# A layer's norm weight moved into its weight blocks, and rows turned by a product with a diagonal matrix

## The reference

```
for l in range(2):
    h = x * rsqrt(mean(x*x, -1) + 1e-6) * pre_norm_g[l]
    l == 0:  proj = h @ w_in_ab;  y = concat(diff_attention * silu(ga), sliding_window * silu(gb)) @ w_out_ab
    l == 1:  proj = h @ w_in_c    (q, k, v, gate: 4 x 1024 columns)
             y = (chunked attention of 16 heads, band of 9 chunks, relative bias) * silu(gate) @ w_out_c
    x = x + (y * rsqrt(mean(y*y, -1) + 1e-6) * post_norm_g[l])
```

## Time and profile before

| what | value |
|---|---|
| median of 3 runs | 1218.73 us (1218.23 to 1219.78) |
| the profiled execution's own time | 1218.22 us |
| its span | 1216.4 us |
| granted PE clock, mean | 0.995 of full speed |
| PE, DVE, ACT, POOL busy | 1186.4, 805.5, 589.1, 432.4 us |
| L2013 (scaling by DVE) | 8 instructions, median 1282 ns |
| L1162 and L1189 (turns) | 32 + 32 transposes, about 273 ns each, overlapped |
| DMA, mean | 64 GB/s |

### The profile page before, as it was taken

One profiled execution on the slowest core, in us unless ns is written; L12 is line 12 of the kernel. 1 busy time (PEld: TensorE's weight loads), 2 busy tenths in 40 slices (PEclk: granted clock), 3 DMA queues, 4 the chain that ended last, 5 costly groups with the idle time before them and its releaser, 6 DMA issues.

```text
span 1216.4 us, 17708 instructions
## 1 busy us (share of the span) xinstructions
PE 1186.4 (98%) x6520; PEld 1011.3 (83%) x6520; DVE 805.5 (66%) x1710; ACT 589.1 (48%) x1296; POOL 432.4 (36%) x557
## 2 busy tenths in 40 slices
PE   9999999999999999898999999999999999999995
PEld 8988888888888887787788888888888888888874
DVE  5464765756667668867554866857658568485677
ACT  6554444434444556655454544544435444345464
POOL 5433214133163464646752214124141241222312
PEclk9999999999999999999999999999999999999998
DMA  6261101011031153235121102011020110201107
GB/s 200 71 188 47 59 18 52 19 52 35 19 87 53 53 156 105 70 114 156 65 78 51 50 19 74 18 57 53 18 74 19 57 53 19 73 19 31 44 20 136
DMA packets 93560, 78.42 MB, mean 64 GB/s; under 512 B 3074, under 2 KB 83970, under 8 KB 93475
## 3 DMA queue, kind: packets, MB, share of 16 engines
q1 hardware_dynamic: 92466, 73.63, 19.9%
q0 software_dynamic: 1008, 3.67, 1.8%
HBM read 68.85 MB, written 13.68 MB: 68 GB/s over the span
## 4 chain that ended last, share of the span: by engine, by line
PE 47%; DVE 2%; ACT 1%; POOL 1%; issue 1%; DVEq 0%; ACTq 0%; POOLq 0%
PE dense L1126 26%; PE dense L1137 7%; PE pv_ps L1259 6%; PE scores L1339 4%; PE turned L1306 4%; PE turned L1294 0%; DVE pT_lo L1844 0%; DVE fin L2040 0%; POOL w_lo L978 0%; ACT k_hh L1448 0%; DVE e_sb L1779 0%; POOL rowstat L1004 0%; POOL rowstat L1001 0%; DVE y L1763 0%; ACT junk L1630 0%
## 5 line engine op out<-in xcount | busy, mean ns | idle before, releaser
L1126 PE MATMUL dense<-hT_hi,w_hi 128*128 128x512 f32 x880 | 350.7, 399 | 0.0
L1126 PE MATMUL dense<-hT_lo,w_hi 128*128 128x512 f32 x880 | 344.7, 392 | 0.0
L1126 PE MATMUL dense<-hT_hi,w_lo 128*128 128x512 f32 x880 | 344.2, 391 | 0.0
L971 POOL TENSOR_SCALAR w_hi<-w_f 128x1024 fp32r<-128x1024 f32 x86 | 93.2, 1084 | 642.2 <-PE dense L1126 585.2
L978 POOL TENSOR_TENSOR w_lo<-w_f,w_hi 128x256 fp32r<-128x256 f32 x344 | 266.3, 806 | 7.2
L1455 ACT ACTIVATE e_sb<-e_sb,low 128x256 f32<-128x256 f32 (+7 forms) x256 | 170.3, 665 | 171.5 <-DVE low L1779 169.2
L1488 ACT ACTIVATE pT_hi<-turned 128x640 fp32r<-128x640 f32 (+3 forms) x224 | 117.2, 523 | 165.7 <-PE pv_ps L1259 95.2
L1126 PEld LDWEIGHTS dense<-hT_hi,w_lo 128*128 128x128 f32 x880 | 165.5, 188 | 36.8
L1126 PEld LDWEIGHTS dense<-hT_hi,w_hi 128*128 128x128 f32 x880 | 166.0, 189 | 26.1 <-issue 0.3
L1126 PEld LDWEIGHTS dense<-hT_lo,w_hi 128*128 128x128 f32 x880 | 166.2, 189 | 25.1
L1844 DVE TENSOR_TENSOR pT_lo<-turned,pT_hi 128x640 fp32r<-128x640 f32 (+3 forms) x224 | 133.6, 597 | 39.6 <-ACT pT_hi L1488 39.4
(11 more groups left out here) (213 smaller groups left out, 1804.4 us busy)
## 6 DMA issues: line engine op xcount, KB each, us to landing
w_f<-in_w_in_c SPq DMA_DIRECT2D x37, 512.0 KB, 4.2
w_f<-in_w_in_ab SPq DMA_DIRECT2D x34, 512.0 KB, 3.9
rel_tiles_dram<-rel_rows_dram SPq DMA_DIRECT2D x1, 5120.0 KB, 23.0
bias<-rel_tiles_dram SPq DMA_DIRECT2D x8, 640.0 KB, 5.4
y<-in_x SPq DMA_DIRECT2D x8, 512.0 KB, 7.7
hT_lo_f<-in_x SPq DMA_DIRECT2D x8, 512.0 KB, 7.3
out_x<-y SPq DMA_DIRECT2D x8, 512.0 KB, 3.6
w_f<-in_w_out_c SPq DMA_DIRECT2D x8, 512.0 KB, 3.8
```

The lines of the kernel that those rows point to most:

```text
L971: ts(hi, src, 1.0, 1.0, ALU.mult, ALU.mult).then_inc(w_hi_done, 1)
L1126: last = mm(dense[:, x.n % 2, :], lhs[:, d * P:(d + 1) * P], rhs[:, d, x.f * HALF:(x.f + 1) * HALF], start=i == 0, stop=i == 23)
```

## The change

The column factors go into the weights. `g_pre` no longer holds a broadcast row: eight small DMAs write `pre_norm_g[1]` into its first eight columns, column d holding the 128 factors of tile d. In `split`, for every weight block of layer 2 except those of its output projection, POOL first multiplies the block in place, eight pieces of 128x128, each by its column of factors, and waits for its own last piece before it rounds.

The row factors go into the turning. In place of DVE's scaling ACT copies the 128x128 identity with the row factors as its scale into one of seven places in the rest of `g_pre` (`root_diag`), a diagonal matrix; PE's transposes become ordinary float32 products of the tile of `y` with that matrix, which turn and scale at once.

```diff
+def takes_g(w):
+    return w.u.kind == "C" and w.b != "o"
...
+    def root_diag(r):
+        k = 1 + r % (DT - 1)
+        return g_pre[:, k * P:(k + 1) * P]
...
-                sp.dma_start(g_pre[:], pre_norm_g[1].partition_broadcast(P)).then_inc(s_gpre, 16)
+                for d in range(DT):
+                    sp.dma_start(g_pre[:, d:d + 1], pre_norm_g[1][d * P:(d + 1) * P].rearrange("(p a) -> p a", a=1))\
+                        .then_inc(s_gpre, 16)
...
-        def split(n, hi_slot, slot, loads):
+        def split(n, hi_slot, slot, loads, scaled=0):
...
+            if scaled:
+                if new(s_gpre, 16 * DT):
+                    pool.wait_ge(s_gpre, 16 * DT)
+                for d in range(DT):
+                    part = (slice(None), d // 4, slice(d % 4 * P, (d % 4 + 1) * P))
+                    last = ts(src[part], src[part], g_pre[:, d:d + 1], None, ALU.mult)
+                last.then_inc(w_scaled, 1)
+                if new(w_scaled, scaled):
+                    pool.wait_ge(w_scaled, scaled)
             ts(hi, src, 1.0, 1.0, ALU.mult, ALU.mult).then_inc(w_hi_done, 1)
...
-                    last = nc.tensor.transpose(dense[:, 2, d * P:(d + 1) * P], x_place(x.row)[:, 4 * x.half + d, :], ident[:])
+                    last = mm(dense[:, 2, d * P:(d + 1) * P], by_tile(y[:, x.row, :])[:, 4 * x.half + d, :], root_diag(x.row),
+                              start=True, stop=True)
...
-                    last = nc.tensor.transpose(row_bank(x)[:, d * P:(d + 1) * P], x_place(x.row)[:, d, :], ident[:])
+                    last = mm(row_bank(x)[:, d * P:(d + 1) * P], by_tile(y[:, x.row, :])[:, d, :], root_diag(x.row),
+                              start=True, stop=True)
...
(ACT, after its squares of the same step)
+                    copy(root_diag(r), ident[:], ACT.Copy, scale=rowstat[:, 5, r:r + 1]).then_inc(n_scaled, 1)
...
(DVE)
-                    stt(out=x_place(r), in0=by_tile(y[:, r, :]), scalar=rowstat[:, 5, r:r + 1], in1=by_tile(g_pre[:]),
-                        op0=ALU.mult, op1=ALU.mult).then_inc(n_scaled, 1)
```

More of the change, by code:

```diff
@@ L719, in program @@
     w_loaded = [sem(f"w_loaded{i}") for i in range(7)]
-    w_hi_done, w_ready = sem("w_hi_done"), sem("w_ready")
+    w_scaled, w_hi_done, w_ready = sem("w_scaled"), sem("w_hi_done"), sem("w_ready")
     s_filled, s_hi_out = sem("filled"), sem("hi_out")
@@ L965, in _ @@
         ts, tt = nc.gpsimd.tensor_scalar, nc.gpsimd.tensor_tensor
-        def split(n, hi_slot, slot, loads):
+        def split(n, hi_slot, slot, loads, scaled=0):
             if new(w_loaded[slot], 16 * loads):
                 pool.wait_ge(w_loaded[slot], 16 * loads)
-            src, hi = f32_place(slot), hi_place(hi_slot)
+            src, hi, lo = f32_place(slot), hi_place(hi_slot), lo_place(slot)
+            if scaled:
[7 more added lines that the diff above has]
+                    pool.wait_ge(w_scaled, scaled)
             ts(hi, src, 1.0, 1.0, ALU.mult, ALU.mult).then_inc(w_hi_done, 1)
@@ L973, in split @@
                 pool.wait_ge(w_hi_done, n + 1)
-            lo = lo_place(slot)
             for h in range(2):
@@ L1075, in _ @@
                 freed_by(w.hi_free)
-                split(PRO_SPLITS + w.n, w.hi, w.slot, w.loads)
+                split(PRO_SPLITS + w.n, w.hi, w.slot, w.loads,
+                      1 + sum(1 for o in WEIGHTS if o.n < w.n and takes_g(o)) if takes_g(w) else 0)
     @block.tensor
@@ L1640, in _ @@
                     copy(junk[:], y[:, r, :], ACT.Square, accum_out=rowstat[:, 3, r:r + 1]).then_inc(n_xsq, 1)
+            for n in NORM:
+                r = n.r
+                if s == n.scaled:
+                    if new(n_xr, r + 1):
+                        act.wait_ge(n_xr, r + 1)
+                    if new(n_sum, r + 1):
+                        act.wait_ge(n_sum, r + 1)
+                    copy(root_diag(r), ident[:], ACT.Copy, scale=rowstat[:, 5, r:r + 1]).then_inc(n_scaled, 1)
             for x in FINAL:
```

## The result

The changed kernel takes 1269.11 us (median of 4 runs, 1268.72 to 1269.70), the kernel before 1218.48 us beside it (4 runs, 1217.97 to 1219.78). The ratio is 1.0414, interval 1.0396 to 1.0432: 50.6 us slower, where 2.0 were forecast and 1226.5 was the upper end of the range.

What follows compares the result with a forecast made beforehand. PE, busy 98% of the span, was taken to bound the kernel. B stage -0.2, bridge +2.2, C0 and after 0 gave +2.0 us: 1220.2 on the profiled execution, 1220.7 as median; range 1218.3 to 1226.5.

Steps and rivals of the forecast that it cites:

- the likeliest case: Whole kernel: a little slower, 1220.7 us, with its own range 1219.2 to 1222.2, chance 0.48.
- The product: Layer 2's turns on PE: two records a tile, 0.24 us, 0.14 more than the transpose, 8.9 us over 64 tiles.
- the dear product: Rival: loads not hidden in the turns, 0.40 us a tile, +10 us, 1228.7; chance 0.06.
- B stage, -0.2: Half turns at the B heads: about 4.6 of 5.6 us of waits won, product costs 4.4, net -0.2 us.
- "faster" rival: B stage and bridge: DVE, 10.3 us lighter, takes every PE wait away; 1216.1 us, chance 0.09.
- Price of a piece, 0.30: POOL's 128x128 scaling piece priced by its select at 0.30 us, 2.5 us a block; upper bound 0.6.
- Bridge, +2.2 (up to +4.5): Turns before the first C head: v split late, new PE wait of 1.8 us; +2.2 us, bounds +0.9 to +4.5.
- C0's wait: Head C0: splits of 6.5 us fit into 7.0, no wait; at 4.8 us of scaling two blocks lack 1.9 each.
- From C1 on ... zero: Heads from C1: POOL's idle time hides 93 us of new scaling; zero, bounded by +2.
- POOL decides: Rival: scaling near its upper bound, v split late in the bridge, two C0 stops of 1.9 us; 1226.8, chance 0.18.
- signs of being wrong: Bridge waits of PE gone, POOL pieces of 0.4 us or more, or PE waiting on POOL in C0.

Runs made afterwards that it cites:

- Number 1: Changed kernel without POOL's scaling of the weight blocks (g left out of the result), product with the diagonal kept: 1216.31 us, ratio 0.9978.
- number 10: Changed kernel with POOL's eight pieces multiplying by two constants of 1.0 (g left out of the result): 1225.54 us, 1.006 of the kernel before.
- number 3: Changed kernel with the output block's split queued ahead of the v block's in C2 to C6: 1236.14 us, ratio 1.0140.
- Number 8: Kernel before, with three more POOL passes (times 1.0, in place) over the v block ahead of its split in C2 to C6: 1234.25 us, ratio 1.0133.
- number 4: Changed kernel with POOL scaling a block by two 128x512 products with broadcast factors in place of eight pieces: 1224.44 us, ratio 1.0044.
- number 9: Changed kernel with two 128x512 pieces, each with one column of factors (most factors wrong), in place of eight: 1241.95 us, 1.019 of the kernel before.
- number 6: Changed kernel with a constant 1.0 in place of the column of factors in POOL's eight pieces: 1254.73 us, 1.030 of the kernel before.

## Why the prediction was wrong

The direction of the likeliest case (a little slower) was right, its size was off by 48 us. By its own steps:

- **The product.** Right in kind, two records a tile; 0.22 us a tile by the starts (0.24 taken). What the prediction cites of the Trainium skill (FP8 and Floating Point Precision, TensorE Precision Notes), four passes for a true FP32 product, by which a tile was 0.21, agrees with this, and the dear product (0.40) is not borne out.
- **B stage, -0.2.** The wait of 2.61 went to 0.54 as worked out (0.4 taken), 3.3 of the 5.6 us went and not 4.6. What it left out is that in these traces the clock no longer falls there. Number 1 shows B stage and bridge without scaling together: -2.4 us. That was the "faster" rival's mechanism, as long as POOL does nothing new.
- **Price of a piece, 0.30.** Mis-sized: 0.585. The select that it was read from is another instruction; the upper bound, 0.6, held. The price decides between 1269 and 1225.5 (number 10).
- **Bridge, +2.2 (up to +4.5).** The wait between turns 5 and 6 is there, 3.60 in place of 1.8. Not foreseen was the wait of 5.95 ahead of the turns. In the changed kernel POOL works without a gap from 533.96 to 569.8; the walk began at 575 us and took POOL to be on time at its start. With C0's wait of 1.80 (forecast: none; the upper bound had 1.9) and the clock behind the long ones, these stages cost 19.8 us, by number 3 against number 1.
- **"From C1 on ... zero".** This is the step that failed, with 33 of the 50.6 us. The argument was that POOL's idle time hides the new work. There is such time, 8.4 us ahead of the v split, but it is time in which POOL waits for a semaphore, and the scaling was put behind that wait; behind the scaling stand the v split and then a split that isn't scaled and has a deadline of its own, with 0.7 us of room. Number 8 reproduces it in the kernel before, number 3 removes it, number 10 shows it at the price that was forecast.
- **The clock, in no term.** Some 18 us of the loss is PE at its lower level behind its long waits (changed kernel against number 1); they are part of the 33 and the 19.8. A wait was priced at its length; behind a wait of 4.06 us it costs 6.5.

The rival "POOL decides" had the right mechanism and nearly the right price (0.6 a piece), but looked only at the bridge and C0, and so ended at 1226.8, still 42 us too low. Two of the prediction's own signs of being wrong did show: pieces of 0.4 us or more, and waits of PE on POOL in C0.

## What to carry to other kernels

Work that is put in front of an item of a queue is paid by everything behind it: walk the queue to the next item that somebody waits for, and look how much room that one had, not how idle the engine is. Idle time helps only if the new work stands ahead of the wait in which the engine is idle. Price an operation by a row with the same form of instruction, or measure it; by a mere likeness it can be off by a factor of two. Where a change adds a long wait of TensorE, look in the trace for what the clock did behind waits of that length, and charge that too.

## What the runs showed of the hardware

**The clock behind a wait.** The five waits in C2 to C6, where PE is busy ahead of the wait and behind it, with the mean granted clock in the next 5 us: 1.3 us (number 4), 1.00 five times; 2.27 (number 9), 0.66, 0.66, 0.67, 1.00, 0.66; 2.6 (number 8), 1.00 three times and 0.69, 0.68; 3.36 (number 6), 0.50, 0.67, 1.00, 0.50, 0.71; 4.06 (changed kernel), 0.50 five times. Of number 6:

```profile
770.70:775.90 5.20, 5.20 (x14) 0.50 0.00 0
...
938.70:943.90 5.20, 5.20 (x27) 1.00 0.00 0
```

Of number 9, the first and the fourth:

```profile
764.23:769.23 5.00, 5.00 (x17) 0.66 0.00 0
...
1011.26:1016.26 5.00, 5.00 (x26) 1.00 0.01 3
```

And behind the wait of 1.80 us in C0 of the changed kernel:

```profile
613.62:618.62 5.00, 5.00 (x17) 0.66 0.31 90
```

In number 3 the wait at that place is 1.78 us, and the clock behind it stays at 1.00. So waits between 1.8 and 3.4 us come out either way, at the same code in another head or another kernel, and the longer of them are not always the dearer; what decides there is not shown.

**Forms on POOL.** FP32 input, undisturbed: one operation, in place, 2.5 ns a column and 0.26 us; two operations 0.27 us for 128 columns in place, and 1.05 for the rounding's 1024; a product of two tensors with a broadcast operand, in place, 1.02 for 512. A multiplication by a vector was cheaper as a product of two tensors than as the one with a scalar that it looks like.
